# First loads of a two-layer decoder kernel put in another order: constant tables and weights between the x tiles, positions on GpSimd's queue

## The chip, the cores and the metric

The kernel runs on the 8 cores of one Trainium2 chip. Each core computes one of the 8 sequences of the batch on its own, with the same program and the same weights; the cores exchange nothing. The metric is the device time of the slowest core in microseconds. A core has five engines with a queue of instructions each: TensorE (PE in the rows: matmuls and transposes, PEld: their weight loads), VectorE (DVE), ScalarE (ACT), GpSimd (POOL) and SyncE (SP), which here only issues DMAs. An engine takes its instructions strictly in order; an instruction that waits for a semaphore holds up all that stand behind it on that engine. Sixteen DMA engines do the transfers. Those issued by SyncE run on one queue (q1, hardware_dynamic in the rows), those issued by GpSimd on another (q0, software_dynamic).

## The reference, cut to what matters

```python
# x: (8, 2048, 1024) f32, positions: (8, 2048) int32
# layer 1
h = rms_norm(x, a_norm)
x = x + mamba2_mixer(h, ...)        # in_proj 1024 -> z, x, B, C, dt; conv of width 4; chunked scan; out_proj
x = x + conv_ffn(x, ...)            # 1024 -> 2 x 2816, conv of width 3, SiLU gate, 2816 -> 1024
# layer 2
k, v = split(rms_norm(x, kv_norm) @ w_kv + b_kv)
k = rotary(rms_norm(k, k_norm), positions)
q = rotary(rms_norm(rms_norm(x, b_norm) @ w_q + b_q, q_norm), positions)
x = x + sliding_window_sink_attention(q, k, v, sinks) @ w_o + b_o
x = x + conv_ffn(x, ...)

def rotary(x, positions):           # cos and sin of positions * inv_freq, per token
    ...
def mamba2_mixer(h, in_proj, conv_w, conv_b, ...):
    zxbcdt = h @ in_proj
    z, xBC, dt = split(zxbcdt)
    xBC = silu(causal_dwconv(xBC, conv_w, conv_b))
    ...
```

## The kernel before

A core works on its 2048 tokens in two halves of 1024 (h = 0, 1). The program is built as a list of operations with their dependencies, in the order of the Python code, and a planner in the kernel file then fixes the order on every engine (`schedule`). It gives each operation a first priority from its place in the list, plus `K.boost`, and from the length of the work that depends on it. Then it lays out the whole program forward in time (`forward`: on each engine the ready operation with the lowest priority goes next), lays it out backward from the end (`backward`), takes the starts found there as new priorities, and repeats that 16 times. The best of the 17 forward passes is kept. So a change in a few operations can shift the order anywhere in the program, and `K.boost` acts on the first pass only. Nothing of the planner is edited.

The stages are: layer 1's mixer on half 0 (8 head groups, `P_gen` the projections and convolutions, `S_gen` the scan), the mixer on half 1 together with the feed-forward of half 0, then attention on one half beside the feed-forward of the other, and a last feed-forward. This change touches the very start.

There the first half of x comes in eight tiles of 128 tokens x 1024 f32, xs_146 to xs_153 in the rows (x0 to x7 in the code), issued by SyncE. `normA0` takes four of them at a time: ScalarE squares each tile and sums (L264, junkA), GpSimd makes the factor from the sums of two tiles (L274 and L268, rs), VectorE multiplies (L274, xnA_156 to xnA_163, bf16), TensorE transposes 128 x 128 blocks against the identity matrix in the table cm (L244), and VectorE or ScalarE writes the result out of PSUM, multiplied by the norm's gain from the table cst (L306 or L305, hT_110). Then TensorE multiplies hT_110 with the first three weight tiles wa_55, wa_56, wa_57 (L239; 1 MB each in HBM as f32, turned to bf16 by the DMA, 512 KB in the core's memory), issued by GpSimd, and with the small tile wdt. ScalarE and VectorE make the width-4 convolution from the products: acc = product x tap + bias on ScalarE (L264, acc_123 and acc_124 in turn), two more taps on VectorE (L280), the last added by GpSimd (L268).

Beside that VectorE and ScalarE make the cos and sin tables of the rotary step from the positions (`rope_tables`: rt_posf, rt_ang, rt_kf, rt_posi, rt_tb, about twelve steps of 128 x 512 for each of the two angles), which are needed by attention only, much later. Before the change the positions come in on SyncE's queue as posv.

The weight loads of the first three tiles are held back by `held["A"]`: each `wload` in ring A takes the next entry of that list as one more dependency.

Of the kernel before, what the change touches and what calls it, by code (L numbers as in the profile page):

```python
# [773 lines left out]
def build():  # L774
    K = Builder()
    nc = K.nc

    def din(name, shape, dt=F32):
        return nc.dram_tensor(name, list(shape), dt, kind="ExternalInput").ap()

    x_d = din("x", [T, D])
    pos_d = din("pos", [1, T], I32)
# [6 lines left out]
    W_d = {k: din(k, [128, n]) for k, n in WSHAPES.items()}  # L789
# [11 lines left out]
    def alloc(name, shape, dt):  # L801
        t = K.sb(name, shape, dt, cur[0])
        nb = int(np.prod(shape[1:])) * DT_SIZE[dt]
        cur[0] += (nb + 31) // 32 * 32
        return t
# [32 lines left out]
    def C(name, j=None, n=None):  # L838
        o, w = CST[name]
        if j is None:  # L840
            return cst[:, o:o + w]
        return cst[:, o + j:o + j + (n or 1)]
# [8 lines left out]
    held = {"A": [], "F": []}  # L851
# [34 lines left out]
    def run(g):  # L886
        for _ in g:
            pass
# [57 lines left out]
    wdt = alloc("wdt", [128, 8, 32], BF16)  # L946
# [20 lines left out]
    xs = [K.sb(f"xs{i}", [128, 1024], F32, (X0 + 16384 + 4096 * i) if i < 4 else (Y1 + 4096 * (i - 4))) for i in range(8)]  # L967
# [12 lines left out]

    posv = K.sb("posv", [128, 512], I32, X1)
    for q in range(4):
        K.dma("sp", posv[32 * q:32 * q + 32, :], pos_d[0:1, q * 512:(q + 1) * 512].partition_broadcast(32), f"pos{q}")
    xdma = [K.dma("sp", xs[i][:], x_d[i * 128:(i + 1) * 128, :], f"x{i}") for i in range(4)]
    K.dma("sp", cm[:], cm_d[:, 0:768], "c1")
    K.dma("sp", cst[:], cst_d, "c0")
    xdma += [K.dma("sp", xs[i][:], x_d[i * 128:(i + 1) * 128, :], f"x{i}") for i in range(4, 8)]
    K.dma("sp", hmb[:], cm_d[:, 768:1280], "c5")
    K.dma("sp", cf[:], cf_d, "c2")
    K.memset(nhalf[:], -0.5)  # L990
    K.memset(epsb[:], EPS)
    o = K.dma("pool", wdt[:], W_d["wdt"].rearrange("p (a b) -> p a b", a=8), "c4")
    K.after(o, xdma[3])
    held["A"].extend([xdma[3], xdma[7], xdma[7]])

    abank = [0]

    def nextA():
        b = 4 + abank[0] % 4
        abank[0] += 1  # L1000
        return b
# [17 lines left out]
    def setup_A():  # L1019
        K.act(avec[:], C("alog"), AF.Exp)  # L1020
        K.ts(avec[:], avec[:], -1.0, None, OP.mult)
        K.act(esk[:], C("sink"), AF.Exp)
        K.copy(Dhb[:], C("Dc"))
        K.tt(Dlo[:], C("Dc"), Dhb[:], OP.subtract)
        for b in range(2):
            K.memset(ARb[b][:], 1.0, eng="pool")
            K.memset(LTb[b][:], 0.0, eng="pool")
            for cc in range(4):
                K.memset(LTb[b][32 * cc:32 * cc + 12, :, cc, :], 1.0)

    def dt_half(h):
        b = nextA()
        pd = ps[0:64, b, :]
        if h == 0:
            K.memset(rmask[:], 1.0, eng="pool")
            K.memset(rmask[:].rearrange("p (c l) -> p c l", c=4)[:, :, 0:1], 0.0, eng="pool")
        for j in range(2):
            for kc in range(8):
                K.mm(ps[32 * j:32 * j + 32, b, :], wdt[:, kc, :], hT[h][:, kc, j * 512:(j + 1) * 512],
                     start=(kc == 0), stop=(kc == 7))  # L1040
        v0, dt, ac, nv, v4 = [v[:] for v in dtv]
        K.act(v0, pd, AF.Exp, bias=C("dtb")[0:64, :])
        K.act(dt, v0, AF.Ln, bias=1.0)
        K.ts(v0, dt, avec[0:64, :], None, OP.mult)
        K.ts(v4, dt, 1e-19, None, OP.max)
        K.scan(ac, rmask[:], v0, 0.0, OP.mult, OP.add)
        K.act(v4, v4, AF.Ln)
        K.tt(nv, v4, ac, OP.subtract)
        for src, AH in ((ac, AHa), (nv, AHn)):
            K.copy(AH[:, 0, :], src)  # L1050
            K.tt(v4, src, AH[:, 0, :], OP.subtract)
            K.copy(AH[:, 1, :], v4)
            K.tt(v4, v4, AH[:, 1, :], OP.subtract)
            K.copy(AH[:, 2, :], v4)
        for scr, AH, s in ((scr_a, AHa, "sa"), (scr_n, AHn, "sn")):
            for j in range(2):
                K.dma("sp", scr[h].ap()[:, :, j * 512:(j + 1) * 512], AH[32 * j:32 * j + 32, :, :], f"{s}{h}{j}")
        aend = ac.rearrange("p (c l) -> p c l", c=4)[:, :, 127:128].to_broadcast([64, 4, 128])
        K.tt(nv.rearrange("p (c l) -> p c l", c=4), nv.rearrange("p (c l) -> p c l", c=4), aend, OP.add)
        K.act(v0, ac, AF.Exp)  # L1060
        K.act(nv, nv, AF.Exp)
        b2 = nextA()
        pv = ps[:, b2, :].rearrange("p (c s j e) -> p c s j e", c=4, s=2, j=2)
        for cc in range(4):
            for s, src in ((0, v0), (1, nv)):
                K.tr(ps[:, b2, (cc * 2 + s) * 64:(cc * 2 + s + 1) * 64], src[:, cc * 128:(cc + 1) * 128], identf[0:64, 0:64])
        for s in range(2):
            K.copy(tokS[:, h * 8:(h + 1) * 8, s * 32:(s + 1) * 32].rearrange("p (j c) e -> p j c e", j=2),
                   pv[:, :, s, :, :].rearrange("p c j e -> p j c e"))
        b3 = nextA()  # L1070
        K.mm(ps[:, b3, 0:256].rearrange("p (c e) -> p c e", c=8), sel127, tokS[:, h * 8:(h + 1) * 8, 0:32])
        K.copy(cdec[:, h * 8:(h + 1) * 8, :], ps[:, b3, 0:256].rearrange("p (c e) -> p c e", c=8))
# [268 lines left out]
    def A_gen(i0, i1):  # L1341
        for i in range(i0, i1):
            if i in (4, 5, 6, 7):
                held["F"].append(K.all_ops[-1])
            if i == 1:
                gain_row(growA[:], "a")
            if i in (1, 2):
                normA1(i - 1)
            if i == 3:
                dt_half(1)  # L1350
            if i == 7:
                halo_taps()
            gens = [(boosted(S_gen(i), SB), 10.4)]
            if i + 1 < len(units):
                gens.insert(0, (P_gen(i + 1), 27.8 if 3 <= i + 1 < 8 else (13.8 if i + 1 > 10 else 20.8)))
            yield from inter(*gens)
# [119 lines left out]
    for i in range(2):  # L1476
        a = alloc(f"qraw{i}", [128, 512], F32)
        b = alloc(f"qrs{i}", [128, 512], F32)
# [199 lines left out]
    normA0()  # L1678
    setup_A()
    run(P_gen(0))  # L1680
    dt_half(0)
    run(A_gen(0, 8))
    K.mark("A1+F00")
# [37 lines left out]
```

How the kernel before makes its waits and increments, by code:

```python
        def run(eng, e):  # L595
            nw = 0
            for op in self.ops[eng]:
                for k, v in plan[op]:
                    e.wait_ge(sems[k], v)
                    nw += 1
                ins = op.fns[eng](e)
                if op.signal:
                    ins.then_inc(sems[op.semkey if op.dma is not None else eng], op.inc)
            if eng == "sp":
                for k in final_waits:
                    if k in cnt:
                        e.wait_ge(sems[k], cnt[k])
            stats[eng] = (len(self.ops[eng]), nw)
```

## Time and profile before

| | |
|---|---|
| median of 3 runs | 1955.26 us (1952.32 to 1955.56) |
| the profiled execution | 1955.56 us |
| its span, slowest core (core 2) | 1954.2 us |
| span of the other cores | 1932.2 to 1951.7 us |
| TensorE busy | 1807.1 us, 92% |
| VectorE, ScalarE, GpSimd busy | 1324.9, 1133.7, 787.7 us |
| TensorE's mean granted clock, core 2 | 0.976 |

Busy shares are means over stages with different limits. Rows of the timeline give the start in the span, the duration, the engine, the line of the kernel file, the operation, and what it writes and reads; in brackets stands how long the engine had stood idle before, and what ended that.

### The profile page before, as it was taken

Reading aid. Unit: us, or ns where it says so; the run is one execution under the profiler, and the core shown is the slowest. Engines: PE = TensorE matmul, PEld = TensorE weight load, DVE = VectorE, ACT = ScalarE, POOL = GpSimd, SP = SyncE. Lnnn points to the kernel's source line nnn. Section 1 sums busy time; section 2 is a strip of 40 time slices with the busy share of each in tenths; the row PEclk is TensorE's granted clock in tenths of the full one; section 3 lists DMA queues with packets and bytes.
Section 4 is the critical chain, followed back from the end, with each engine's and each line's share of the span. In section 5 each row is a group of like instructions: output and inputs, shape, how many; then the busy total and the mean of one; then the engine's idle time right before and its main releaser. Section 6 shows DMA issues by size and latency. Waiting matters only on the chain.

```text
span 1954.2 us, 30336 instructions; the slowest of 8 cores (1932.2 to 1954.2 us)
## 1 busy us (share of the span) xinstructions
PE 1807.1 (92%) x9795; PEld 895.3 (46%) x9980; DVE 1324.9 (68%) x1997; ACT 1133.7 (58%) x1562; POOL 787.7 (40%) x967
## 2 busy tenths in 40 slices
PE   5779888898999999998799999998999999999999
PEld 3445556544544544444344454344433543444444
DVE  6787868856776898888767556666666566655522
ACT  6778688664765566666447256565774567433310
POOL 3577567723423444345744012624445145200000
PEclk9999899998999999999899999999999999999999
DMA  8665375793656475658644455444543553374444
GB/s 201 121 113 105 61 130 88 115 124 67 114 77 104 85 131 99 107 104 176 174 76 75 77 88 91 76 73 73 86 76 63 92 89 65 47 164 76 76 71 134
DMA packets 155434, 193.72 MB, mean 99 GB/s; under 512 B 106640, under 2 KB 114320, under 8 KB 155280
## 3 DMA queue, kind: packets, MB, share of 16 engines
q0 software_dynamic: 33984, 121.19, 38.2%
q1 hardware_dynamic: 121296, 70.58, 16.7%
q8 instruction: 84, 1.38, 0.3%
q14 instruction: 70, 0.57, 0.1%
HBM read 272.00 MB, written 17.83 MB: 148 GB/s over the span
## 4 chain that ended last, share of the span: by engine, by line
PE 76%; DVE 8%; issue 6%; DMA 5%; ACT 3%; POOL 1%; SPq 1%; DVEq 0%; ACTq 0%; POOLq 0%
PE ps L239 75%; PE ps L244 1%; DVE acc_123 L280 1%; DMA xk_131<-xc_128 1%; DMA wf_60<-wout 1%; DMA xk_131<-xc_127 1%; DVE acc_124 L280 1%; DMA cm<-cm 1%; DMA wf_61<-wfin 1%; ACT L264 1%; DMA wf_58<-wout 1%; DMA xk_132<-xc_127 1%; SPq L318 1%; DMA scrst<-prevF_91 0%; DVE yn_83 L274 0%
## 5 line engine op out<-in xcount | busy, mean ns | idle before, releaser
L264 ACT ACT_TABLE_LOAD x188 | 241.2, 1283 | 112.6 <-PE ps L239 38.6
L239 PE MATMUL ps<-hF,wf_59 128*128 128x512 bf16 x533 | 136.9, 382 | 2.4 <-DVE uF L268 1.1
L280 DVE SCALAR_TENSOR_TENSOR facc_181<-ps,cst,facc_181 128x1023 f32<-128x1023 f32 x88 | 112.5, 1279 | 36.7 <-ACT facc_181 L264 33.8
L239 PE MATMUL ps<-hF,wf_58 128*128 128x512 bf16 x532 | 132.2, 379 | 1.6 <-DVE uF L268 0.7
L280 DVE SCALAR_TENSOR_TENSOR facc_182<-ps,cst,facc_182 128x1023 f32<-128x1023 f32 x88 | 112.4, 1278 | 26.4 <-ACT facc_182 L264 24.5
L239 PE MATMUL ps<-hF,wf_60 128*128 128x512 bf16 x498 | 124.0, 380 | 2.0 <-DVE hrawF L295 1.0
L239 PE MATMUL ps<-hF,wf_61 128*128 128x512 bf16 x501 | 123.9, 379 | 1.7 <-DVE uF L268 0.8
L280 DVE SCALAR_TENSOR_TENSOR acc_124<-ps,cst,acc_124 128x1023 f32<-128x1023 f32 (+2 forms) x80 | 101.8, 1273 | 11.0 <-ACT acc_124 L264 9.7
L280 DVE SCALAR_TENSOR_TENSOR acc_123<-ps,cst,acc_123 128x1023 f32<-128x1023 f32 (+2 forms) x80 | 101.9, 1273 | 9.8 <-ACT raw_144 L264 6.1
L264 ACT ACTIVATE facc_181<-ps,cst 128x1024 f32<-128x1024 f32 x44 | 52.9, 1203 | 55.8 <-PE ps L239 55.6
L239 PE MATMUL ps<-wa_56,hT_110 128*128 128x256 bf16 x512 | 68.8, 292 | 14.9 <-DVE acc_123 L280 7.8
L239 PEld LDWEIGHTS ps<-hF,wf_59 128*128 128x128 bf16 x544 | 52.4, 98 | 64.0 <-issue 7.9
L239 PEld LDWEIGHTS ps<-hF,wf_58 128*128 128x128 bf16 x544 | 52.3, 98 | 62.1 <-issue 2.7
L239 PE MATMUL ps<-wf_61,uF 128*128 128x512 bf16 x259 | 79.8, 379 | 0.6 <-issue 0.2
L239 PE MATMUL ps<-wf_60,uF 128*128 128x512 bf16 x255 | 78.5, 379 | 0.3
L239 PE MATMUL ps<-wf_58,uF 128*128 128x512 bf16 x254 | 76.6, 379 | 2.1 <-DVE uF L268 1.1
L239 PE MATMUL ps<-wf_59,uF 128*128 128x512 bf16 x261 | 78.2, 379 | 0.3
L264 ACT ACTIVATE sg_184<-facc_182 128x1024 bf16<-128x1024 f32 x44 | 46.5, 1056 | 53.6 <-DVE facc_182 L268 47.1
L264 ACT ACTIVATE sg_183<-facc_181 128x1024 bf16<-128x1024 f32 x44 | 46.5, 1056 | 52.3 <-DVE facc_181 L268 38.7
L239 PEld LDWEIGHTS ps<-hF,wf_60 128*128 128x128 bf16 x512 | 48.9, 98 | 58.4 <-issue 5.6
L239 PEld LDWEIGHTS ps<-hF,wf_61 128*128 128x128 bf16 x512 | 48.4, 98 | 59.5 <-issue 6.7
L264 ACT ACTIVATE facc_182<-ps,cst 128x1024 f32<-128x1024 f32 x44 | 52.8, 1200 | 34.8 <-PE ps L239 34.7
(570 smaller groups left out, 4689.2 us busy)
## 6 DMA issues: line engine op xcount, KB each, us to landing
wf_58<-wfin POOLq DMA_DIRECT2D x22, 512.0 KB, 5.9
wf_59<-wfin POOLq DMA_DIRECT2D x22, 512.0 KB, 5.9
wf_60<-wfin POOLq DMA_DIRECT2D x22, 512.0 KB, 5.6
wf_61<-wfin POOLq DMA_DIRECT2D x22, 512.0 KB, 6.6
wa_55<-wA POOLq DMA_DIRECT2D x15, 512.0 KB, 7.9
wa_56<-wA POOLq DMA_DIRECT2D x14, 512.0 KB, 6.6
wa_57<-wA POOLq DMA_DIRECT2D x14, 512.0 KB, 6.7
wf_58<-wfdn POOLq DMA_DIRECT2D x9, 512.0 KB, 5.3
```

The source lines that it names most:

```text
L239: return self.add("pe", lambda e: e.matmul(out, lhsT, rhs, start=start, stop=stop, **kw), [lhsT, rhs] + ([] if start else [out]), [out], c)
L244: return self.add("pe", lambda e: e.transpose(out, in_, ident), [in_, ident], [out], c)
L264: return self.add("act", lambda e: e.activation(out, in_, func, **kw), rd, wr, c, table=table)
L280: return self.add(eng, lambda e: e.scalar_tensor_tensor(out, in0, scalar, in1, op0, op1), rd, [out], c)
L318: return self.add(queue, lambda e: e.dma_start(out=out, in_=in_), [in_], [out], 0.55 if queue == "pool" else cost, dma_sem=sem, nbytes=nb)
```

## The change

The positions are issued by GpSimd in place of SyncE. The x tiles, cm and cst get priorities that make them the first things of all in the planner's first pass, in the order x0, x1, x2, cm, x3, cst, x4 to x7, hmb, cf; x5, x6 and x7 wait for x1, x2 and x3 to have landed. The three first weight tiles wait for x0, x2 and x4 instead of x3, x7 and x7. wdt loses its wait for x3 and moves in the list to behind the first projections.

```diff
     for q in range(4):
-        K.dma("sp", posv[32 * q:32 * q + 32, :], pos_d[0:1, q * 512:(q + 1) * 512].partition_broadcast(32), f"pos{q}")
-    xdma = [K.dma("sp", xs[i][:], x_d[i * 128:(i + 1) * 128, :], f"x{i}") for i in range(4)]
+        K.dma("pool", posv[32 * q:32 * q + 32, :], pos_d[0:1, q * 512:(q + 1) * 512].partition_broadcast(32), f"pos{q}")
+    xdma = []
+    first = [0]
+
+    def lead():
+        first[0] += 1
+        K.boost = -10 ** 6 + 10 ** 4 * first[0]
+
+    def load_x(i):
+        lead()
+        xdma.append(K.dma("sp", xs[i][:], x_d[i * 128:(i + 1) * 128, :], f"x{i}"))
+        if i > 4:
+            K.after(xdma[i], xdma[i - 4])
+
+    for i in range(3):
+        load_x(i)
+    lead()
     K.dma("sp", cm[:], cm_d[:, 0:768], "c1")
+    load_x(3)
+    lead()
     K.dma("sp", cst[:], cst_d, "c0")
-    xdma += [K.dma("sp", xs[i][:], x_d[i * 128:(i + 1) * 128, :], f"x{i}") for i in range(4, 8)]
+    for i in range(4, 8):
+        load_x(i)
+    lead()
     K.dma("sp", hmb[:], cm_d[:, 768:1280], "c5")
     K.dma("sp", cf[:], cf_d, "c2")
+    K.boost = 0
     K.memset(nhalf[:], -0.5)
     K.memset(epsb[:], EPS)
-    o = K.dma("pool", wdt[:], W_d["wdt"].rearrange("p (a b) -> p a b", a=8), "c4")
-    K.after(o, xdma[3])
-    held["A"].extend([xdma[3], xdma[7], xdma[7]])
+    held["A"].extend([xdma[0], xdma[2], xdma[4]])
+
+    def load_wdt():
+        K.dma("pool", wdt[:], W_d["wdt"].rearrange("p (a b) -> p a b", a=8), "c4")
...
     run(P_gen(0))
+    load_wdt()
     dt_half(0)
```

What the planner makes of it is seen on the engines' queues. First SyncE, from its fourth DMA on; before:

```order
L318 DMA xs_149<-x 128x1024
L318 DMA xs_150<-x 128x1024
L318 DMA xs_151<-x 128x1024
L318 DMA xs_152<-x 128x1024
L318 DMA xs_153<-x 128x1024
L318 DMA cm<-cm 128x768
L318 DMA cst<-cst 128x439
L318 DMA posv<-pos 32x512 x4
L318 DMA cf<-cf 128x256
L318 DMA hmb<-cm 128x512
```

The same place on SyncE now:

```order
L318 DMA xs_149<-x 128x1024
L318 DMA xs_150<-x 128x1024
L318 DMA cm<-cm 128x768
L318 DMA cst<-cst 128x439
L318 DMA cf<-cf 128x256
L318 DMA hmb<-cm 128x512
L318 DMA xs_151<-x 128x1024
L318 DMA xs_152<-x 128x1024
L318 DMA xs_153<-x 128x1024
```

All four tables have moved ahead of the last three tiles, and the positions are gone from this queue.

GpSimd behind its memsets (LT_120 and prevF_92 are the last of them), up to the last of the three first weight tiles; before:

```order
L311 MEMSET LT_120 128x1024
L311 MEMSET prevF_92 128x256
L274 TENSOR_SCALAR rs<-ssq 128x2
L268 TENSOR_TENSOR rs<-rs,nhalf 128x2
L274 TENSOR_SCALAR rs<-ssq 128x2
L268 TENSOR_TENSOR rs<-rs,nhalf 128x2
L318 DMA wa_55<-wA 128x2048
L318 DMA wdt<-wdt 128x256
...
L318 DMA wa_56<-wA 128x2048
L318 DMA wa_57<-wA 128x2048
```

GpSimd now, where four loads of posv and wdt already stand ahead of the memsets:

```order
L311 MEMSET LT_120 128x1024
L318 DMA wa_55<-wA 128x2048
L274 TENSOR_SCALAR rs<-ssq 128x2
L268 TENSOR_TENSOR rs<-rs,nhalf 128x2
L318 DMA wa_56<-wA 128x2048
L274 TENSOR_SCALAR rs<-ssq 128x2
L268 TENSOR_TENSOR rs<-rs,nhalf 128x2
L318 DMA wa_57<-wA 128x2048
```

The weight loads have moved in between the norm's small steps, one to four steps earlier than before.

VectorE at the second angle of the rotary tables (rt_ang from rt_posf onward) and the first convolution steps (acc_123); before:

```order
L280 SCALAR_TENSOR_TENSOR acc_124<-ps,cst,acc_124 128x1022
L274 TENSOR_SCALAR Dd_138<-cm,Dlo 128x128
L280 SCALAR_TENSOR_TENSOR xnA_164<-xq_154,rs,growA 128x1024
L275 TENSOR_SCALAR rt_ang<-rt_posf,cst 128x512
L274 TENSOR_SCALAR rt_kf<-rt_ang 128x512
L295 CAST rt_posi<-rt_kf 128x512
L295 CAST rt_kf<-rt_posi 128x512
L280 SCALAR_TENSOR_TENSOR rt_ang<-rt_kf,rt_ang 128x512 x2
L280 SCALAR_TENSOR_TENSOR xnA_165<-xq_155,rs,growA 128x1024
L280 SCALAR_TENSOR_TENSOR acc_123<-ps,cst,acc_123 128x1023
```

VectorE now, from the last normalized tile to the very first convolution step:

```order
L274 TENSOR_SCALAR xnA_163<-xs_153,rs 128x1024
L275 TENSOR_SCALAR rt_ang<-rt_posf,cst 128x512
L306 TENSOR_SCALAR hT_110<-ps,cst 128x512 x4
L274 TENSOR_SCALAR rt_kf<-rt_ang 128x512
L295 CAST rt_posi<-rt_kf 128x512
L295 CAST rt_kf<-rt_posi 128x512
L280 SCALAR_TENSOR_TENSOR rt_ang<-rt_kf,rt_ang 128x512 x2
L275 TENSOR_SCALAR rt_kf<-rt_ang 128x512
L268 TENSOR_TENSOR rt_ang<-rt_ang,rt_kf 128x512
L280 SCALAR_TENSOR_TENSOR acc_123<-ps,cst,acc_123 128x1023
```

Before, these steps stood behind the first four convolution steps; now they stand ahead of the first.

On TensorE the 64 transposes stood in one row ahead of all matmuls on wa_55. Now the second half of them comes in between:

```order
L239 MATMUL ps<-hT_110,wa_55 128x512 x5
L244 MATMUL ps<-cm,xnA_160 128x128 x4
L244 MATMUL ps<-cm,xnA_161 128x128 x4
L239 MATMUL ps<-hT_110,wa_55 128x512 x11
L244 MATMUL ps<-cm,xnA_162 128x128 x4
L244 MATMUL ps<-cm,xnA_163 128x128
```

Sixteen of the 32 matmuls of the first tile's first two blocks have moved ahead of the last transposes.

## Rows read from the trace of the kernel before

**Rows 1.** Stretches: busy PE, PEld, DVE, ACT, POOL (count), clock, DMA share, GB/s
```profile
0.00:100.00 100.00, 68.48 (x408) 40.44 (x415) 71.88 (x119) 71.21 (x88) 46.44 (x58) 0.97 0.76 161
...
900.00:1000.00 100.00, 82.66 (x399) 35.68 (x406) 76.70 (x121) 52.71 (x99) 70.51 (x68) 0.90 0.74 166
...
1100.00:1200.00 100.00, 99.47 (x495) 47.56 (x504) 53.52 (x79) 45.71 (x56) 15.38 (x23) 1.00 0.54 91
```
**Rows 2.** TensorE's waits, whole span: who for whom, us in total, times, longest
```profile
PE ps L244 <- DMA cm<-cm: 19.1, 1, 19.1
PE ps L239 <- DVE acc_123 L280: 11.5, 6, 4.1
```
**Rows 3.** Timeline, 5 to 21 us, the loads and the first norm
```profile
5.88 0.66 SPq L318 DMA_DIRECT2D cm<-cm  x1
...
9.42 0.22 POOL L274 TENSOR_SCALAR rs<-ssq 128x2 f32<-128x2 f32 x1 [4.68 <-ACT junkA_142 L264]
...
13.03 1.06 ACT L264 ACTIVATE junkA_141<-xs_150 128x1024 bf16<-128x1024 f32 x1 [0.29 <-DMA xs_150<-x]
...
13.94 1.02 POOL L318 DMA_DIRECT2D wa_55<-wA  x1
...
14.75 0.75 DVE L274 TENSOR_SCALAR xnA_159<-xs_149,rs 128x1024 bf16<-128x1024 f32 x1
...
18.29 1.06 ACT L264 ACTIVATE junkA_142<-xs_153 128x1024 bf16<-128x1024 f32 x1 [0.23 <-DMA xs_153<-x]
...
19.09 0.26 PE L244 MATMUL ps<-cm,xnA_156 128*128 128x128 bf16 x1 [19.09 <-DMA cm<-cm]
...
20.64 0.60 POOL L318 DMA_DIRECT2D wa_56<-wA  x1
```
**Rows 4.** Timeline, 26 to 75 us, first convolutions and rotary steps
```profile
27.27 7.45 PE L239 MATMUL ps<-hT_110,wa_55 128*128 128x512 bf16 x31 [0.22 <-issue]
...
31.37 1.21 ACT L264 ACTIVATE acc_123<-ps,cst 128x1024 f32<-128x1024 f32 x1 [2.54 <-PE ps L239]
...
34.96 0.42 DVE L275 TENSOR_SCALAR rt_kf<-rt_ang 128x512 f32<-128x512 f32 x1
...
51.20 0.68 DVE L268 TENSOR_TENSOR rt_ang<-rt_ang,rt_kf 128x512 f32<-128x512 f32 x1
...
69.43 4.98 PE L239 MATMUL ps<-wa_56,hT_110 128*128 128x256 bf16 x29 [4.06 <-DVE acc_123 L280]
```
**Rows 5.** DMA from 10 to 14 us: packets, MB; queue's share of 16 engines
```profile
DMA packets 360, 1.30 MB, mean 326 GB/s; under 512 B 42, under 2 KB 42, under 8 KB 360
...
q1 hardware_dynamic: 360, 1.30, 102.6%
```
**Rows 6.** Stretches with the columns of rows 1, around the VectorE-bound part
```profile
33.69:69.43 35.74, 27.16 (x152) 14.82 (x153) 34.89 (x46) 31.66 (x37) 17.16 (x17) 0.95 0.70 140
50.00:60.00 10.00, 7.00 (x40) 4.83 (x42) 10.00 (x12) 8.58 (x12) 5.56 (x4) 0.83 0.97 165
69.43:75.22 5.79, 5.74 (x35) 4.24 (x37) 5.27 (x8) 3.90 (x4) 4.18 (x2) 0.71 0.92 159
```
**Rows 7.** DMA issues, 0 to 60 us: count, KB each, median us to landing
```profile
posv<-pos SPq DMA_DIRECT2D x4, 64.0 KB, 13.2
...
cm<-cm SPq DMA_DIRECT2D x1, 192.0 KB, 13.1
...
wdt<-wdt POOLq DMA_DIRECT2D x1, 64.0 KB, 9.8
```
**Rows 8.** The chain that ended last, at the first transposes: start, us, what
```profile
19.09 3.65 PE ps L244 x32
```
**Rows 9.** DMA from 24 to 26 us, the weight queue
```profile
q0 software_dynamic: 101, 0.38, 104.2%
```
**Rows 10.** DMA from 16 to 18 us, the only queue with packets
```profile
q1 hardware_dynamic: 269, 0.51, 92.4%
```

## The prediction

> **What bounds the kernel now.** I read the stretches of 100 us first. TensorE is busy 68.5 us of the first 100 and 99.5 us of the stretch from 1100 [rows 1]: the start is the emptiest place of the program, and it is what the edited lines set. The list of TensorE's waits names the reasons. The longest single one is 19.1 us for cm, the table with the identity that every transpose needs; the next name is acc_123, VectorE's convolution sums, with 11.5 us in six waits, the longest 4.1 [rows 2]. The timeline shows the first wait from inside. cm is issued at 5.88 us, behind eight x tiles of 512 KB, and the first transpose runs at 19.09, although the first four normalized tiles are complete at 15.5 (xnA_159, 14.75 + 0.75). The first matmul on a weight tile comes at 27.27 and the first convolution on ScalarE at 31.37 [rows 3, 4]. The transfers are the bound up to here: from 10 to 14 us the hardware queue fills the engines (102.6%, 326 GB/s) [rows 5].
>
> From 33.69 to 69.43 us another engine is the bound. VectorE is busy 34.89 of 35.74 us, ScalarE 31.66, TensorE 27.16 [rows 6]. TensorE's 4.06 us wait for acc_123 stands at the end of this stretch [rows 4]. So a gain at the start is worth only what VectorE and ScalarE let through.
>
> **The change, part by part.** The profiled execution took 1955.56 us, its span is 1954.2, and the median of the three runs shown is 1955.26: the sum is made against the execution and carried to the median by 0.3 us.
>
> *Tables between the tiles.* In the order the change really gives, cm stands behind five tiles, not three as the code's text has it: the boost enters the first planning pass only, and the printed order puts xs_150 ahead of cm. The fifth tile is there at 13.0 us (its square starts at 13.03) [rows 3]. After it come cm with 192 KB, and in between the positions (four loads of 64 KB) and wdt (64 KB) [rows 7], now on GpSimd's queue from the first microsecond. That is 0.52 MB, at 326 GB/s 1.6 us: cm lands at about 14.6. Transposes then start some 4 us earlier, and the first 32 of them (3.65 us [rows 8]) are over at about 18.5 instead of 22.7. By itself that is worth nothing, for the second half of the tiles goes the other way.
>
> *The last tiles.* Six loads (cm, cst, cf, hmb, positions, wdt: 987 KB together, cm the row shown) now stand in front of tile xs_153. At 326 GB/s they take 3.1 us, and its landing moves from 18.2 to 21.3. The waits of x5 to x7 on x1 to x3 cost nothing, since those have landed before the queue's backlog is through. What counts is wa_55 and wa_56, now issued behind x0 and x2, at about 8.6 and 10.5 us instead of 13.94 and 20.64. A weight tile takes 2.8 us of all engines: 0.38 MB in 2 us at 104.2% for a tile of 0.52 MB [rows 9]. If the weights wait for the x tiles, xs_153 lands at 21.3; if both go ahead, at 26.9; I take one of them ahead, 24.1. The rows lean to waiting: wa_55's issue began at 13.94 [rows 3], and from 16 to 18 us the hardware queue still had 92.4% of the engines' time and the software queue no packet [rows 10]. But at 21.3 wa_55 itself would land at 24.1, and the change puts 16 of its matmuls in front of the last transposes, so that this end is no better than the middle.
>
> The Trainium skill speaks against this edit: "DMA: Bandwidth & Descriptors", section "Queues, rings and completion order", says that each DMA engine takes turns between the queues it has work for, packet by packet. By that, both weight tiles get in among the x tiles and the landing is the 26.9 end. The 16 to 18 us row does not show such turns, the stretch behind it does not exclude them; the rule's result is the second rival below.
>
> After xs_153: its square 1.25 us with the read of the sum, GpSimd's two small steps 0.95, two casts of 0.75, the last 20 transposes 2.3 (0.114 each [rows 8]), an evacuation 0.7, and the eight matmuls of the first channel block, 1.9 (7.45 us for 31 [rows 4]), with 0.3 to ScalarE's start: 8.9 us. So the first convolution starts at 33.0 instead of 31.37: **+1.6 us** (from -1.2 at 21.3 with the weights in time, to +4.4 at 26.9).
>
> *Rotary tables moved ahead.* Because VectorE stands idle while the tiles come, the new order puts ten steps of the rotary tables, from the compare at 34.96 to the sum at 51.20, ahead of its first convolution step. By their rows they last 0.42 + 0.68 + 0.61 + 0.47 + 3 x 0.43 + 1.50 + 0.42 + 0.68 = 6.1 us (first and last shown [rows 4]). All of it comes out of a stretch in which VectorE has 0.85 us to spare. ScalarE caps the gain: it has 4.1 us to spare there, and loses one 0.62 us sine step to the start. **-4.7 us**, between 0 (ScalarE's order gives nothing) and -6.1.
>
> *The clock.* TensorE's granted clock is 0.71 in the 5.79 us behind the 4.06 us wait, which is a mix of 1.2 and 2.4 GHz; 0.29 x 5.79 = 1.7 us are lost there, and as much from 50 to 60 us at 0.83 [rows 6]. A relief of 4.7 covers the 4.06 us wait, so I take the one loss as gone: **-1.7 us** (0 to -3.4).
>
> *Positions and wdt on GpSimd.* Five issues of some 0.6 us (the first weight issue took 1.02 [rows 3]) put 3.5 us in front of 3.7 us of memsets, so GpSimd is free at about 8.6; its first norm step came at 9.42 [rows 3]. The cover is 0.8 us; behind it stands now wa_55's issue, 1.0, so the first tiles' scales are perhaps 0.3 late. cm at 14.6 hides that. If GpSimd were 5 us later, the first transposes would wait for it.
>
> *Everything else.* The planner runs its passes anew, and the order of all engines differs down to the last stage. Counts stay: as many matmuls, 188 activation-table loads before and after by the sequence of functions, five evacuations moved from VectorE to ScalarE. No row says which way this goes. TensorE's idle from 900 to 1000 us alone is 17.3 us [rows 1]; I put 0 for all of it, with 6 us either way, a third of that stretch.
>
> Sum: +1.6 - 4.7 - 1.7 = -4.8 us, 1950.8 in the profiled execution's terms, **1950.5** for the median.
>
> **The rivals.**
> *The relief is taken by ScalarE.* It is busy 31.66 of 35.74 us and starts 1.6 us later; none of its activation-table loads in that stretch goes. Then the 4.7 shrink to about 1.6, the wait of TensorE stays, with its clock: 1955.3, no change that can be told. Against it: part of ScalarE's idle time there is waiting for VectorE's sums through GpSimd, which come sooner.
>
> *The weights take the place of the tiles.* Weight tiles wa_55, wa_56 and also wa_57 (now issued behind x4, at about 14 us) go ahead of xs_153: it lands at 24.1 + 2 x 2.8 = 29.7, the first convolution starts 7.2 us late, the relief of 4.7 stands against it, and TensorE waits between the two halves long enough to come back at the lower level, a loss like that of the row at 0.71: +7.2 - 4.7 + 1.7 = +4.2, **1959.5**. It decides from a landing at 28.9 on, where +1.6 + 4.8 is used up. For it: the weight loads are issued 5 to 10 us earlier into a queue that is full. Against it: the row from 16 to 18 us.
> The skill's rule of turns, named above, would bring 26.9 or later here, the lower half of this case.
>
> *The rest of the order loses.* If the stretch from 900 to 1000 us, or several smaller ones, wait half as long again, 8.7 us, the -4.8 turns into +3.9, and more makes it slower: about 1961. The same luck the other way gives 1945.
>
> *The change doesn't do what it says* holds in part, as the order shows (cm behind five tiles), and is in the sum.
>
> **How the numbers follow.** The forecast, front gained and the rest even: 0.45. ScalarE takes the relief: 0.29. Weights in front: 0.10. The rest loses: 0.11; the rest wins: 0.05. A measurement of this kernel can tell about 0.2%, 3.9 us, from no change. Faster by more: 0.45 + 0.05 = 0.50; within: 0.29; slower by more: 0.21. The forecast's own range is 1944 to 1957, from the bounds of its terms. The range for 8 in 10 must take in the weights' case and about half of what the rest may do on either side: 1943 to 1961.
>
> **What would show it.** In the new profile: the first transpose at about 14.6 us; xs_153's square at 24 us, with 21.3 or 27 to 30 telling which queue went first; the first convolution of ScalarE at 33; then, up to the place where TensorE's second block on wa_56 starts (69.43 before), an arrival at 63 to 66 us and a last wait for acc_123 well under 4 us. If that place is not reached sooner, the relief was not worth its price. If it is, and the span is no shorter, the later stages gave it back, and the stretches of 100 us will say where. A transpose start at 19 us or later would make the first step wrong.

## The result, and the profile after

The changed kernel takes **1939.41 us** (1938.83 to 1940.94) against 1953.79 us for the kernel before on the same chip: a ratio of 0.9928, 95% interval 0.9911 to 0.9945. That is 14 us faster, below the lower end of the range. The sign is the forecast one, but hardly anything of the forecast's sum is behind it: the start of the program, from which the gain was to come, has become 12 us *slower*, and the gain is made in stages whose code the change doesn't touch. Ratios, here and below, leave out executions in which the cores of a die show a lower granted clock than the others, which makes any of these kernels some per cent slower.

The profiled execution took 1938.83 us, the slowest core's span (core 5) is 1937.7, the others' 1928.1 to 1937.7. The median of the eight cores went from 1941.6 to 1932.1 (9.4 us); the rest of the slowest core's 16.5 us is that the cores lie closer together.

The stretches first, with the columns of [rows 1]. The kernel after:

```profile
0.00:100.00 100.00, 62.63 (x366) 35.60 (x367) 69.95 (x118) 64.04 (x80) 43.27 (x58) 0.97 0.70 158
200.00:300.00 100.00, 89.08 (x661) 56.49 (x658) 76.30 (x138) 78.90 (x118) 67.01 (x74) 0.91 0.51 99
300.00:400.00 100.00, 91.72 (x708) 59.51 (x709) 83.63 (x140) 78.34 (x119) 73.58 (x93) 0.98 0.72 122
400.00:500.00 100.00, 94.06 (x572) 49.53 (x569) 65.00 (x114) 59.66 (x87) 34.65 (x51) 0.98 0.49 91
900.00:1000.00 100.00, 89.28 (x392) 37.38 (x392) 65.29 (x98) 53.48 (x96) 61.56 (x56) 0.95 0.62 142
```

Three of these stretches of the kernel before, which were not shown ahead of the prediction:

```profile
200.00:300.00 100.00, 83.31 (x628) 54.87 (x637) 76.77 (x133) 76.75 (x112) 62.39 (x72) 0.93 0.52 93
300.00:400.00 100.00, 87.57 (x651) 56.02 (x660) 81.33 (x129) 73.33 (x114) 69.53 (x89) 0.97 0.75 105
400.00:500.00 100.00, 88.35 (x521) 46.85 (x530) 62.14 (x116) 57.11 (x83) 33.03 (x50) 0.93 0.61 95
```

In the first 100 us TensorE is busy 62.63 us where it was 68.48 [rows 1]: 6 us less work done. From 200 to 500 it is busy 274.9 us where it was 259.2: 16 us more, in the stage that runs the mixer's scan beside other work.

How this adds up over the program is read best from TensorE's work itself. The table is worked out from the matmul records of the traces: at which time has TensorE done a given share of all its columns, median of the eight cores, minus the same for the kernel before. The head of a column is the time at which the kernel before is there; +12 means 12 us late, and a column's difference to its neighbour is what that part of the program cost or gained. Each line is one execution. From one execution of a kernel to the next the median core's span varies with a standard deviation of mostly 1 to 3 us, and e4's line is the fastest of three executions (1924.2, 1928.3 and 1935.2), so the table alone doesn't show differences of a few us between lines. The column at 979 is the least certain: values change by up to some 10 us within 5 us of it.

```
us of before      39    130    230    476    873    979   1081   1904
after          +12.4   +4.2   -0.4  -16.0  -13.6  -20.4   -8.9   -9.3
e1             +12.6  +11.5  +12.0  +10.5  +11.6  +10.5  +11.9  +12.4
e2             +13.4  +10.5   +4.1   -7.3   -5.8  -12.2   -0.3   -1.1
e3              -0.2   -1.3   -7.2  -20.3  -16.6  -22.6   -9.6  -10.4
e4              -0.3   -1.7  -15.6  -30.9  -27.2  -24.1  -17.3  -17.2
e5              +4.8   +4.6   +4.3   +0.7   +2.2   +3.4   +3.9   +3.9
e6             +10.2   +9.0   +9.6   +6.8   +6.7  +10.7  +10.3  +10.3
e7             +12.6   +5.2   +0.1  -14.8   -1.2   +1.0   +0.6   -0.8
e8              -0.4   -0.5   -0.8   -4.6   -1.2   -9.2   +4.0   +3.5
e9               0.0   -1.9  -15.1  -31.9  -24.3  -24.4  -24.5  -24.7
e10             -0.4   -2.2   -9.4  -21.5  -19.4  -25.5  -14.7  -14.7
e11             -0.4   -0.9   -6.4  -13.8   -8.1   -1.7   +7.8   +7.2
e12            +13.9   +6.9   +0.9   -9.9   -4.2   -1.7   +2.7   +2.5
```

The first line is the change: 12.4 us lost by 39 us, 26 us won between there and 873, 4.7 lost again up to 1081, and nothing in the last 800 us. The bulge of 20.4 at 979 is in every kernel that has the changed order there (after, e2, e3, e8, e10), and 11 to 13 us of the lead at 979 are gone 100 us later. In part it is other work taken first: at 960 us the changed kernel has done some 5600 columns more of the mixer's out-projection (`wf,yT`) and as many fewer of attention's products, mostly its query projection (`hq,wa`). At 990 the same products are done in both, the lead is still 19 us, and half of it goes by 1040. So it is not all work taken ahead; what takes the rest back is not shown, only that TensorE then waits for VectorE's next steps (e10 below).

**The start after.** TensorE's longest waits, as [rows 2]:

```profile
PE ps L244 <- DMA cm<-cm: 20.1, 1, 20.1
...
PE ps L244 <- DVE xnA_160 L274: 4.3, 1, 4.3
```

The wait for cm has grown from 19.1 to 20.1, though cm was issued 1.7 us earlier, and a new wait of 4.3 us between the two halves of the transposes has come. The timeline (columns of [rows 3, 4]):

```profile
4.16 0.48 SPq L318 DMA_DIRECT2D cm<-cm  x1
...
7.91 0.57 POOL L318 DMA_DIRECT2D wa_55<-wA  x1
8.10 0.33 SPq L318 DMA_DIRECT2D xs_151<-x  x1
...
11.84 0.73 POOL L318 DMA_DIRECT2D wa_56<-wA  x1 [1.26 <-DMA xs_148<-x]
...
13.66 0.33 SPq L318 DMA_DIRECT2D xs_153<-x  x1
...
17.02 0.70 POOL L318 DMA_DIRECT2D wa_57<-wA  x1 [0.94 <-DMA xs_150<-x]
...
31.39 1.06 ACT L264 ACTIVATE junkA_142<-xs_153 128x1024 bf16<-128x1024 f32 x1
...
33.60 1.14 POOL L268 TENSOR_TENSOR rs<-rs,nhalf 128x2 f32<-128x2 f32 x1
...
37.94 0.75 DVE L274 TENSOR_SCALAR xnA_163<-xs_153,rs 128x1024 bf16<-128x1024 f32 x1
...
43.09 1.20 ACT L264 ACTIVATE acc_123<-ps,cst 128x1024 f32<-128x1024 f32 x1 [1.17 <-PE ps L239]
...
77.51 3.36 PE L239 MATMUL ps<-wa_56,hT_110 128*128 128x256 bf16 x15 [4.04 <-DVE acc_123 L280]
```

The weight loads leave GpSimd at 7.91, 11.84 and 17.02, in the middle of the x tiles. The last tile is squared at 31.39 (18.29 before [rows 3]), the first convolution on ScalarE comes at 43.09 (31.37 before [rows 4]), and the place that stood at 69.43 [rows 4] at 77.51, behind a wait of 4.04 us that was 4.06. TensorE's mean granted clock from there to 84.04 is 0.60, a mix of its two levels (1.2 and 2.4 GHz), where it was 0.71 [rows 6]: the loss of clock behind this wait has stayed too.

```profile
77.51:84.04 6.53, 6.53 (x40) 4.82 (x40) 5.89 (x6) 3.42 (x4) 4.61 (x4) 0.60 0.52 88
```

The DMA queues from 14 to 16 us, as [rows 5, 10]:

```profile
DMA packets 132, 0.39 MB, mean 195 GB/s; under 512 B 11, under 2 KB 52, under 8 KB 132
...
q0 software_dynamic: 68, 0.28, 93.5%
q1 hardware_dynamic: 64, 0.11, 18.3%
```

The packets are about as many on the weight queue as on the other, 68 and 64, but the weight packets take 93.5% of the engines' time. That is 16 engines x 2 us x 0.935 / 68 = 0.44 us for one of them, and 0.09 us for one of the others; most of the others are smaller, though (52 packets are under 2 KB). The equal counts agree with the rule of the Trainium skill that the prediction weighed ("DMA: Bandwidth & Descriptors", section "Queues, rings and completion order": turns between queues, packet by packet), if a packet of the profile is one in the page's sense, which no run here shows. Turns by packet are no turns by time when one queue's packets last longer.

### The profile page after: what moved, and what is told of

It is laid out like the page before. It is cut to its first block, busy times and chain, and to the rows that moved or that the text cites. A ratio compares the mean times of both kernels' runs of the same rounds, so it can differ in the third digit from the quotient of the medians.

```text
span 1937.7 us, 30513 instructions; the slowest of 8 cores (1928.1 to 1937.7 us)
## 1 busy us (share of the span) xinstructions
PE 1813.8 (94%) x9980; PEld 890.4 (46%) x9980; DVE 1315.9 (68%) x1992; ACT 1136.5 (59%) x1567; POOL 786.0 (41%) x971
## 4 chain that ended last, share of the span: by engine, by line
PE 81%; DVE 6%; issue 5%; DMA 4%; ACT 2%; POOL 2%; SPq 0%; DVEq 0%; POOLq 0%; ACTq 0%
PE ps L239 79%; PE ps L244 1%; DMA xs_151<-x 1%; DMA xk_131<-xc_128 1%; DVE acc_123 L280 1%; DVE acc_124 L280 1%; DVE dtv_170 L268 0%; DMA wf_58<-wout 0%; DMA xk_132<-xc_127 0%; POOL xdd_133 L268 0%; DMA xk_132<-xc_128 0%; DMA xs_147<-x 0%; ACT L264 0%; POOL grs L268 0%; DVE t_87 L268 0%
## 5 line engine op out<-in xcount | busy, mean ns | idle before, releaser
L239 PE MATMUL ps<-hF,wf_59 128*128 128x512 bf16 x544 | 137.5, 383 | 0.7 <-DVE uF L268 0.4
L239 PE MATMUL ps<-hF,wf_58 128*128 128x512 bf16 x544 | 133.9, 379 | 0.7 <-DVE uF L268 0.7
L239 PE MATMUL ps<-hF,wf_60 128*128 128x512 bf16 x512 | 126.8, 381 | 1.1 <-DVE hrawF L295 1.0
L239 PE MATMUL ps<-hF,wf_61 128*128 128x512 bf16 x512 | 125.4, 379 | 0.9 <-DVE uF L268 0.8
L239 PE MATMUL ps<-wf_60,uF 128*128 128x512 bf16 x264 | 80.6, 379 | 0.0
L239 PE MATMUL ps<-wf_61,uF 128*128 128x512 bf16 x264 | 80.5, 379 | 0.0
L239 PE MATMUL ps<-wf_58,uF 128*128 128x512 bf16 x264 | 78.9, 379 | 1.1 <-DVE uF L268 1.1
L239 PE MATMUL ps<-wf_59,uF 128*128 128x512 bf16 x264 | 79.4, 379 | 0.0
L239 PE MATMUL ps<-wa_56,hT_110 128*128 128x256 bf16 x512 | 64.6, 281 | 11.7 <-DVE acc_123 L280 8.8
```

The costliest lines, as they stand in the source:

```text
L239: return self.add("pe", lambda e: e.matmul(out, lhsT, rhs, start=start, stop=stop, **kw), [lhsT, rhs] + ([] if start else [out]), [out], c)
```

## The experiments

The reading above is the theory: the new loads cost time, and the gain is the planner's new order of everything behind them. The rivals: that the loads bring the gain in a way the start doesn't show, and that the change makes a better order by something it does, not by chance. In the kernels e1 to e3 and e5 to e10 the order of every engine is put together from two planned programs (KF, KR) of the same operations: `make(True)` has the loads of the change, `make(False)` those of before, and `start` is an operation's planned time.

**e1: the loads alone.** The loads of the change at the start, every other instruction in the order of before.

```diff
+LOADS_NEW = True
...
+    KF = make(LOADS_NEW)
+    KR = make(not LOADS_NEW)
...
+        order[e] = head + [byk[kr[op]] for op in KR.ops[e]
...
+    impose(KF, order)
```

> Only the first loads are as in the change (queues, order and waits of the x tiles, tables, positions and first three weight tiles); every other instruction stands in the order of the kernel before. Theory A (the new loads are a cost at the start, and the gain is the order that the planner found for the rest): slower than before, 1957 to 1964 us, xs_153 squared at 28 us or later and the first product group some 8 us late. Theory B (the loads carry the gain): 1938 to 1945 us.

Ratio 1.0069 (1.005 to 1.0089): 14 us slower, a little more than expected. The line of the table is flat: 12.6 us lost by 39 us, 12.4 at the end. So the loads by themselves cost 12 us, with nothing given back.

**e2: the order alone.** The loads of before at the start, everything else in the order of the changed kernel: e1 with `LOADS_NEW = False`.

> The other way round: the loads of before, every other instruction in the order of the changed kernel. Theory A: faster than the changed kernel by what the loads cost, 1929 to 1937 us. Theory B: back at before, 1950 to 1956 us.

Ratio 0.997 (0.9952 to 0.9988): a miss, less of a gain than the theory wanted. The table says why: it is 13.4 us late at 39 us as well. The changed order of the start was planned for its own loads; with the old ones, in which the positions come late on SyncE's queue, VectorE's cast of the positions stands ahead of xnA_158 and holds it up:

```profile
23.93 0.43 DVE L295 CAST rt_posf<-posv 128x512 f32<-128x512 int32 x1 [12.22 <-DMA posv<-pos]
```

From 39 to 873 us it wins 19 us. A front and its loads can't be exchanged apart, so the next cut is in time.

**e3: the start of before, then the order after.** Operations that before plans in the first 60 us keep before's order and loads; all others take the changed kernel's.

```diff
+CUT = 60.0
+FRONT_NEW = False
...
+    front = {op for op in KF.all_ops if op.start < CUT}
+    order = {e: [op for op in KF.ops[e] if op in front] for e in KF.ENGS}
...
+            if op not in front:
+                order[e].append(op)
```

> Every instruction that the planner of before starts in its first 60 us stands as in before, loads too, and all others in the order of the changed kernel. Theory A: the start of before is 8 to 13 us ahead at the first products, so 1928 to 1935 us. Theory B: 1950 to 1956 us. If the steps moved ahead in the changed order are what helps later, between the two, 1937 to 1945.

Ratio 0.9918 (0.9896 to 0.9939), 2 us above the range of theory A. The whole gain is there with none of the change's loads. Taking the start's 12.4 us away again brought 1.1 us at the end, though: the difference to the changed kernel is 12.6 us at 39, 6.8 at 230, 4.3 at 476 and 1.1 at 1904. By the ratios of the two kernels the difference at the end is 2 us, give or take 5. So the cost of the loads depends on what follows: 12 us with before's order behind (e1), a few at most with the new order behind. The parts don't add up: +12.4 for the loads alone (e1) and -10.4 for the order alone (e3) would be +2, and the change has -9.3. What in the new order absorbs the cost was not found.

**e4: another order, no change at all.** The kernel before, one constant of the planner at 21 in place of 20: by how much lower an operation's priority must be before ScalarE's activation table is switched for it in the plan.

```diff
-    pen_f = 20.0
+    pen_f = 21.0
```

> The kernel before with one number of the planner changed, the cost of a table switch in its forward passes 21 for 20; the loads are those of before. It gives another order of about the same planned length. Theory A (the gain is one draw among orders): a time that differs from before by more than 4 us either way, up to 15. Theory B: within 3 us of before.

Ratio 0.994 (0.992 to 0.9959), with the loads of before, and 188 table loads as before. A redrawn order of the same program is worth about as much as the whole change. It leads by 31 us at 476 and loses 10 between 873 and 1081.

**e5 and e6: which loads cost.** e5 has the tables, x tiles and positions of the change but the weights as before; e6 the loads of before but the three weight tiles released by x0, x2, x4. Both in the order of before, except that e6 issues the weight tiles at the change's places among the norm's steps. The decisive line of e5, against e1:

```diff
-        held["A"].extend([xdma[0], xdma[2], xdma[4]])
+        held["A"].extend([xdma[3], xdma[7], xdma[7]])
```

> The order of before, with the new loads but for the weights: cm, cst, cf and hmb ahead of the last three x tiles, these three waiting for earlier ones, the positions on GpSimd's queue; the three weight tiles and wdt are issued where before issues them. Theory A1 (the early weights take the DMA engines from the x tiles, that is the 12 us of the loads alone): cm lands near 15 us, xs_153 near 22, 1948 to 1957 us. Theory A2 (the tables ahead of the last tiles and the waits are the cost): xs_153 at 26 us or later, 1958 to 1967 us.

Ratio 1.0032 (1.0007 to 1.0057), 4 to 5 us late at the start and 4 at the end. And e6, against before:

```diff
-    held["A"].extend([xdma[3], xdma[7], xdma[7]])
...
+        held["A"].extend([xdma[0], xdma[2], xdma[4]] if early else [xdma[3], xdma[7], xdma[7]])
...
+    KF = make(False, True)
```

> The order and the loads of before, but the first three weight tiles wait for x0, x2 and x4 and stand in GpSimd's order where the change puts them. Theory A1: the x tiles behind the first two land 6 us late or more, cm at 23 us or later, 1960 to 1967 us. Theory A2: within 3 us of before, 1950 to 1956.

Ratio 1.0045 (1.0032 to 1.0058), 10 us late at the start and at the end. The wait for cm, e5 and then e6:

```profile
PE ps L244 <- DMA cm<-cm: 15.4, 1, 15.4
```

```profile
PE ps L244 <- DMA cm<-cm: 29.4, 1, 29.4
```

And the squares of the last three tiles in e6, each with ScalarE's idle time ahead of it, ended by the tile's landing:

```profile
19.12 1.06 ACT L264 ACTIVATE junkA<-xs 128x1024 bf16<-128x1024 f32 x1 [3.50 <-DMA xs<-x]
...
23.83 1.06 ACT L264 ACTIVATE junkA<-xs 128x1024 bf16<-128x1024 f32 x1 [3.55 <-DMA xs<-x]
...
27.81 1.06 ACT L264 ACTIVATE junkA<-xs 128x1024 bf16<-128x1024 f32 x1 [2.83 <-DMA xs<-x]
```

The last of them in e5:

```profile
23.49 1.06 ACT L264 ACTIVATE junkA<-xs 128x1024 bf16<-128x1024 f32 x1 [2.23 <-DMA xs<-x]
```

Without the early weights cm is there at 15.4, close to the 14.6 of the prediction; with them alone, and cm still behind the tiles, at 29.4. The early weights are most of the price, and moving the tables ahead costs, too: in e5 the last tile is squared at 23.5 us (18.29 before [rows 3]), 5.2 us later, where the prediction gave their bytes 3.1. Whether the waits of x5 to x7 on earlier tiles, which e5 keeps, are part of this no run separates.

**e7: the start and middle after, the end before.** As e3, with `CUT = 450.0` and `FRONT_NEW = True`.

> What the planner of the changed kernel starts in its first 450 us stands as in the changed kernel, loads too; all others in the order of before. The changed kernel is 18 us ahead of before at this place and 9 at the end (medians of the cores). If the lead of that place is kept, the end is better than the changed kernel's: 1932 to 1938 us. If the stages behind it give it back whatever their order, 1939 to 1945.

Ratio 1.0008 (0.999 to 1.0026): neither of the two expectations. The lead of 14.8 us at 476 is down to 1.2 at 873. Most of it goes right behind the cut: 8 us between 500 and 510. TensorE has done the same products at 476 in both kernels, so this lead was not its own work taken ahead; it then waits for the scan on VectorE (TensorE's waits, 475 to 520 us):

```profile
PE ps L239 <- DVE E L268: 5.5, 1, 5.5
```

**e8: the start and middle before, the end after.** As e3, with `CUT = 450.0`.

> The other cut: before, loads too, up to 450 us of the plan, then the order of the changed kernel. If the gain of the changed order is made ahead of 450 us, and its later part is the worse one, slower than before, 1955 to 1963 us. If the later part is good by itself, 1938 to 1950.

Ratio 1.0015 (0.9996 to 1.0035), between the two expectations. A lead of at most 5 us up to 873, and 5 us lost from there to 1081. In after, e2 and e3 the same order loses 4.7 to 7 us there; before's order loses 0.3 to 3.6 in e1, e5, e6 and e7, and nothing in e9. So the order of before looks like the better one in this part, by a few us.

**e9: the best parts together.** e4's order up to 850 planned us, before's from there, loads of before.

```diff
+    KF = make(False)
+    KR = make(False)
+    KR.pen_f = 21.0
...
+    front = {byk[kk[op]] for op in KR.all_ops if op.start < CUT}
```

> The instruction order of e4 (loads of before, one constant of the planner at 21 in place of 20) up to 850 planned us (about 890 us of the run), and the order of before from there. e4 led before by 28 us at 884 us and by 17 at the end (medians over the cores). Theory D (the time of a stretch belongs to the order of that stretch, and a lead goes on to the next): the lead of about 28 us at 884 stays, the end comes at 1926 to 1934. Rival S (a lead is taken back behind a seam, as e7's was: 16 us of lead at 479 became 1 at the end): 1942 to 1953, with the loss inside 100 us of the seam.

Ratio **0.988** (0.9843 to 0.9917), as theory D had it. The lead is 24.3 us at 873 and 24.7 at the end: here it is passed on whole. Its profiled execution took 1922.15 us. It is the fastest kernel of this study and beats the kernel before; against the changed kernel (0.9911 to 0.9945) the intervals still touch. Stretches of e9, columns as above:

```profile
200.00:300.00 100.00, 90.31 (x701) 59.63 (x700) 80.97 (x137) 82.05 (x120) 69.18 (x80) 0.97 0.58 103
...
1000.00:1100.00 100.00, 98.76 (x467) 44.16 (x468) 60.50 (x77) 43.17 (x50) 23.57 (x29) 0.98 0.43 73
```

**e10: before, after, before.** Before up to 60 planned us, the changed order to 940, before's from there.

```diff
+    mid = {byk[kk[op]] for op in KR.all_ops if op.start < CUT2} - front
```

> The loads and order of before to 60 planned us, the order of the changed kernel to 940 (about 985 us of the run), and the order of before from there. e3, which keeps the changed kernel's order to the end, led by 20 us at 991 and by 10.5 at 1094 and at the end. Theory D: without the changed kernel's order between 991 and 1094 the 20 us stay; 1932 to 1936, 2 to 5 us below e3. Rival S: the lead is lost around the seam; 1937 to 1950.

Ratio 0.9949 (0.9908 to 0.9989). A miss by the slowest core, and by the lead: its 25.5 us at 979 fall to 14.7 at 1081 although before's order is back. TensorE's longest wait from 990 to 1045 us:

```profile
PE ps L244 <- DVE xnF L274: 5.2, 4, 2.0
```

The loss near 1000 us had been put down to the order behind 991; but from 873 to 1081 e10 loses 4.7 us, as much as the changed kernel. The ratio is of the slowest core, whose lag behind the others differs from execution to execution. The median core, over the executions, is 16.0 us ahead of before's, and e3's 12.5: e10 is 3.5 us better, as the cut was to make it, though hardly clear of the scatter.

**e11 and e12: two more draws.** Another constant (how early a load of GpSimd's queue is planned; 3.0 in both kernels), in the kernel before and in the changed kernel.

```diff
-    swdge_slack = 3.0
+    swdge_slack = 2.8
```

> The kernel before with another constant of the planner at 2.8 in place of 3.0 (how early a load of the GpSimd queue is planned); the loads at the start as before. Its planned length is 1871.9 where before's is 1868.5. Theory D (the time is a draw of the planner's order, with a spread of some 10 us between draws of equal planned length): off before's 1953 by more than 4 us, to either side, 1935 to 1965. Rival O (before's order is the usual result and e4 was a lucky one): 1949 to 1957.

```diff
-    swdge_slack = 3.0
+    swdge_slack = 3.2
```

> The changed kernel with the same constant at 3.2 in place of 3.0; the loads at the start as in the changed kernel. Its planned length is 1870.7 where the changed kernel's is 1865.7. Theory D: the gain of 14 us belongs to the one order that the planner kept, so another order of the same change moves it by more than 4 us: 1930 to 1935 or 1944 to 1967. Rival O (the early loads bring about a better order by themselves): 1936 to 1943.

e11: 1.0033 (1.0008 to 1.0058). e12: 0.9993 (0.9966 to 1.0021). Both plans switch ScalarE's activation table 192 times where before, after and e4 have 188; what these four loads cost no run shows. So with the loads of before three orders give 1, 0.994 and 1.0033, and with the loads of the change two give 0.9928 and 0.9993. e12 has the change whole, and its gain is gone. Five draws are too few to tell whether the change makes good orders more likely; they show that it doesn't make one each time. e11 shows where a draw loses, TensorE's waits from 900 to 1100 us:

```profile
PE ps L239 <- DVE att L268: 7.8, 2, 7.4
PE ps L239 <- DVE vA L268: 7.0, 1, 7.0
```

Two attention steps come late on VectorE there, and TensorE stands for 7 us behind each; its stretch from 900 to 1000 is at 73.74 us busy, where before had 82.66 [rows 1]. Ahead of each stand VectorE instructions that lasted many times longer than usual (yn is four of 0.28 us otherwise, qT one of 0.69), beside work on GpSimd almost without a break:

```profile
922.63 6.93 POOL L268 TENSOR_TENSOR x<-x,bob 128x1024 f32<-128x1024 f32 x3
922.88 9.73 DVE L274 TENSOR_SCALAR yn<-yg,grs 128x256 bf16<-128x256 bf16 x4 [0.18 <-POOL grs L268]
...
982.69 6.28 DVE L268 TENSOR_TENSOR qT<-qrs,qraw 128x512 bf16<-128x512 f32 x1
985.05 3.36 POOL L268 TENSOR_TENSOR P<-P,cm 128x512 bf16<-128x512 bf16 x3
...
989.73 0.69 DVE L268 TENSOR_TENSOR qT<-qrs,qraw 128x512 bf16<-128x512 f32 x1
```

So an order also decides which VectorE steps meet GpSimd's work, and the planner has fixed costs for them. In the traces the time that VectorE loses by stretched instructions (all that last over 0.5 us above the usual) goes with the end of the table: 99 to 103 us on the median core in e3, e4, e9 and e10, which lead by 10 us or more, 115 in before, 122 in e11. That is a correlation, over kernels that share parts of their orders; no run here changes this alone.

## Why the prediction was wrong, point by point

**"Everything else: 0 with 6 us either way"** is the step that failed. On the median core the changed kernel won 26 us between 39 and 873 and lost 4.7 behind, -22 together; with the start of before the same order is worth -10.4 (e3). Either is beyond the 6. The bound was a third of the idle of one stretch of 100 us, but the order was redrawn in the whole of the first 1100. What much of the gain is made of can be read: TensorE's largest waits from some 180 us to the same place of the work (476 us before, 460 after). Before:

```profile
PE ps L239 <- DVE acc_124 L280: 5.4, 4, 3.4
PE ps L239 <- DVE prevF_92 L268: 4.6, 3, 2.3
PE ps L239 <- DVE t_88 L268: 4.4, 4, 1.9
PE ps L239 <- POOL xdd_133 L268: 3.7, 2, 2.5
PE ps L239 <- DVE acc_123 L280: 3.7, 2, 3.1
```

After:

```profile
PE ps L239 <- DVE t_87 L268: 6.8, 5, 3.9
PE ps L239 <- DVE E_99 L268: 6.6, 3, 2.7
PE ps L239 <- DVE acc_123 L280: 2.5, 1, 2.5
PE ps L239 <- ACT E_104 L264: 2.1, 3, 1.0
PE ps L239 <- DVE t_88 L268: 1.9, 1, 1.9
```

The waits for the convolution's sums, the carried state (prevF) and the scan's input (xdd) are mostly gone, and others (t_87, E_99) have grown: all waits of the list together went from 39 to 25 us, 14 of the 20 us that these cores won there. Why the new order has fewer of them stays open. The planned length was no guide to the size: it is 1868.5 for before, 1865.7 after, 1870.0, 1871.9 and 1870.7 for e4, e11 and e12; e4's plan, 1.5 longer than before's, ran 12 us shorter.

**The last tiles, +1.6.** Measured +11.7 at the first convolution (43.09 for 31.37). The prediction's middle case let one weight tile ahead of xs_153 and had it land at 24.1; all three went ahead, and it was squared at 31.39, 7.3 us later. The rival "the weights take the place of the tiles" had this mechanism (29.7), and e6 shows it alone. The misreading is that of [rows 10]: no packet of the weight queue from 16 to 18 us was taken as waiting behind the tiles, when the load issued at 13.94 had only not begun: its first packet came at 18.31, 4.4 us after the issue, and in e6, 5.2 us after (5.74 to 10.91), the weights took their turns among the tiles. A row that shows no contention is no evidence of precedence.

**cm at 14.6.** It came at 20.1. The sum of bytes was right (15.4 in e5), but the weights issued at 7.91 and 11.84 were left out of what is in its way. By the prediction's own test, a transpose start at 19 us or later, the first step is wrong.

**From xs_153 to the first convolution, 8.9 us.** Measured 43.09 - 31.39 = 11.7. Of the 2.8 us more some 2.5 are the other edge of the rotary steps: steps of the first angle stand ahead of xnA_162 on VectorE, which starts at 37.28 although GpSimd's factor for it is there at 34.74 (33.60 + 1.14). With the tiles late these steps are on the path, and so are those of the second angle, ahead of VectorE's first convolution step. From the chain of waits, start and duration:

```profile
32.77 0.60 DVE rt_ang L280
...
34.81 0.69 DVE rt_ang L268
...
36.14 0.70 DVE rt_ang L268
...
37.28 0.75 DVE xnA_162 L274
...
43.82 0.70 DVE rt_ang L280
...
45.76 0.14 DVE acc_123 L280
```

The prediction let VectorE do them while it waits for tiles, and did not ask what they hold up when the tiles come late.

**The relief of 4.7 and the clock's 1.7.** From +11.7 at the first convolution the lag falls to +8.1 at the place on wa_56 (77.51 for 69.43): 3.6 us of relief, between the forecast and its rival "ScalarE takes the relief" (1.6). The wait behind it did not shrink (4.04 for 4.06), nor did the clock come back (0.60): the -1.7 is not there.

**Positions and wdt on GpSimd.** On GpSimd itself no delay is seen: wa_55 left at 7.91 where 8.6 was expected.

**The forecast's own range.** The bounds of its terms add up to -10.7 and +4.4, that is 1944.6 to 1959.7 us; the upper end of 1957 is not their sum. The measured time lies below either.

So the forecast's sign was right by luck, for another reason than the one given, and "the rest of the order wins", which had 0.05, is what happened.

## What to carry to other kernels

Where a planner lays the whole program out anew, any edit of its input draws a new order, and here two draws of the same loads lie 0.6 to 0.9% apart, as much as the whole edit brought. Such an edit has to be measured against redraws of the kernel without it (a constant changed by a few per cent), and its own effect with the order of the rest held still: e1 said +0.7% where the change as a whole said -0.7%. Once orders are measured by stretch, parts of two can be joined, and the lead may be kept (e9) or lost behind the seam (e7, and in part e10); the join has to be measured, too.

## What the runs showed of the hardware that was not expected

**A weight load's packets.** From 14 to 20 us of the changed kernel both queues had packets in about equal number (68 and 64, 68 and 84, 70 and 74 in two us each). The weight packets, f32 turned to bf16 on the way, took longer: from 10 to 24 us one of 4 KB took 0.41 us on average on the weight queue and 0.19 on the other. From 10 to 14 us before, with x tiles alone, it was 16 x 4 x 1.026 / 360 = 0.18 us for a packet of 3.6 KB [rows 5]. An early weight load therefore cost the x tiles more than its share of the bytes: in e6 the last three tiles were squared 4.0 to 4.7 us behind the one ahead of each. That is about one x tile, 1.6 us (512 KB at the 326 GB/s of [rows 5]), and one weight tile, 2.8 us by the prediction's estimate from [rows 9].

**VectorE beside GpSimd.** An instruction that lasts 0.69 us otherwise took 6.28 us in e11 while GpSimd worked almost without a break. In the traces of before, after and e11 each core has some 80 to 100 VectorE instructions that last over 0.5 us longer than usual for their shape, and every one of them overlaps GpSimd's work for at least 30% of its time; not every overlap lengthens one.
